# A mixture-of-experts stage on Trainium2: five weight buffers in place of six, and table work moved around the token copies

## What is computed

```
proj = rmsnorm(x) @ w_in
x = x + concat(o_a, o_b, o_c) @ w_out
h = rmsnorm(x)                        # router, then for every expert e:
a = h @ w_e_gate[e]; u = h @ w_e_up[e]
out = out + (silu(a) * u * gate[:, e]) @ w_e_down[e]
return rmsnorm(x + out)
```

## Time and profile before

| | us |
|---|---|
| median of 3 runs | 1177.11 |
| lowest and highest of them | 1172.47, 1177.11 |
| the profiled execution's own time | 1175.49 |
| its span | 1173.7 |

### The profile page before, as it was taken

The page is one execution under the profiler, slowest core; times in us unless marked ns, Lnnn a source line. Parts: engine busy times, 40 slices in busy tenths (PEclk is TensorE's granted clock), DMA queues, the critical chain, the costliest instruction groups (busy, mean ns, idle before and its releaser), DMA issues.

```text
span 1173.7 us, 30645 instructions
## 1 busy us (share of the span) xinstructions
PE 1073.7 (91%) x12370; PEld 912.3 (78%) x12370; DVE 664.3 (57%) x1727; ACT 462.8 (39%) x790; POOL 252.0 (21%) x476
## 2 busy tenths in 40 slices
PE   6999899999999999999999899987989999999980
PEld 5989788778788888888877677777778878888860
DVE  5340445324666666665687533467877755656654
ACT  6321112222455555554587422221334434434333
POOL 1030000000333323321176300001223222323310
PEclk9999899999999999999999999996999999999995
DMA  9020855353656855565332365438899799999927
GB/s 366 20 90 2 292 179 161 108 159 141 160 118 164 205 141 119 127 138 130 105 86 57 120 216 191 135 126 321 285 342 368 229 371 357 356 375 366 366 53 293
DMA packets 77834, 232.92 MB, mean 198 GB/s; under 512 B 23264, under 2 KB 24064, under 8 KB 76544
## 3 DMA queue, kind: packets, MB, share of 16 engines
q1 hardware_dynamic: 70080, 214.18, 55.1%
q0 software_dynamic: 7616, 16.80, 6.3%
HBM read 194.87 MB, written 45.88 MB: 205 GB/s over the span
## 4 chain that ended last, share of the span: by engine, by line
PE 76%; DMA 8%; DVE 6%; issue 4%; ACT 2%; SPq 2%; POOL 1%; POOLq 0%; DVEq 0%; ACTq 0%
PE PS L2382 14%; PE PS L2044 13%; PE PS L2222 9%; PE PS L2306 8%; PE PS L2393 7%; PE PS L2033 6%; PE PS L2200 4%; PE PS L2161 4%; PE PS L2201 3%; DMA wdn<-in_wdn 2%; PE PS L2373 2%; DMA k<-T_d 2%; DMA wst<-in_wt 1%; PE PS L2079 1%; PE PS L2194 1%
## 5 line engine op out<-in xcount | busy, mean ns | idle before, releaser
L2382 PEld LDWEIGHTS PS<-XT,wgu 128*64 128x64 f32 x4352 | 184.9, 139 | 31.0 <-issue 29.1
L1158 ACT ACTIVATE pt<-PS,cst 128x512 f32<-128x512 f32 (+3 forms) x288 | 167.2, 650 | 105.5 <-PE PS L2201 83.3
L2382 PE MATMUL PS<-XT,wgu 128*64 128x96 f32 x4352 | 192.1, 249 | 16.7 <-issue 13.0
L1488 DVE CUSTOM_DVE_ANT_0 junkm<-PS,cst 128x512 f32<-128x512 f32 (+3 forms) x276 | 133.5, 531 | 75.2 <-PE PS L2161 73.0
L2222 PEld LDWEIGHTS PS<-V,pt 128*64 128x64 f32 x3840 | 121.2, 137 | 22.8 <-issue 11.6
L2222 PE MATMUL PS<-V,pt 128*64 128x65 f32 x3840 | 136.8, 225 | 0.7 <-issue 0.7
L2044 PE MATMUL PS<-hTh,wth 128*128 128x512 f32 x256 | 103.0, 402 | 4.8 <-DVE wtl L1335 4.8
L2044 PE MATMUL PS<-hTh,wtl 128*128 128x512 f32 x256 | 100.7, 393 | 0.0
L2044 PE MATMUL PS<-hTl,wth 128*128 128x512 f32 x256 | 100.7, 393 | 0.0
L870 POOL TENSOR_SCALAR_AFFINE_SELECT pt<-pt 128x128 f32<-128x128 f32 x224 | 64.0, 292 | 159.7 <-ACT pt L1158 116.7
L1912 DVE TENSOR_TENSOR wdl<-wdn,wdh 128x1024 fp32r<-128x1024 f32 x64 | 75.5, 1222 | 38.6 <-ACT wdh L999 38.6
(11 more groups left out here) (314 smaller groups left out, 1885.8 us busy)
## 6 DMA issues: line engine op xcount, KB each, us to landing
wgu<-in_wgu SPq DMA_DIRECT2D x32, 2048.0 KB
wdn<-in_wdn SPq DMA_DIRECT2D x32, 1024.0 KB
q<-T_d SPq DMA_DIRECT2D x58, 256.0 KB, 4.3
k<-T_d SPq DMA_DIRECT2D x58, 256.0 KB, 5.5
wst<-in_wt SPq DMA_DIRECT2D x16, 512.0 KB, 6.5
T_d<-thi SPq DMA_DIRECT2D x16, 512.0 KB, 2.7
T_d<-tlo SPq DMA_DIRECT2D x16, 512.0 KB, 3.9
xt<-in_x SPq DMA_DIRECT2D x8, 512.0 KB, 11.3
```

Of the source, the lines that this page charges most:

```text
L1158: ins = nc.scalar.activation(pt[:, (n + 2) % 6, 0:nt * P], PS[:, n % 3, 0:nt * P], ACT.Exp, scale=C("slopes", h, h + 1), bias=C("kb", w, w ...
L1488: V_.tensor_tensor_reduce(out=junk_[:, 0:L], in0=PS[:, bank, 0:L], in1=tab, scale=1.0, scalar=-3e38, op0=ALU.add, op1=ALU.max, accum_out=m ...
L2382: ins = mm(PS[h * HD:(h + 1) * HD, 2 + p, f * CAP:(f + 1) * CAP], wgu[q][:, c, lo:lo + HD], XT[:, p, c, :], start=(c == 0 and f == 0), sto ...
```

## The change

- `RING` goes from 6 to 5: the sixth buffer is gone, `SLOT` is `l % 5` for all loads, and each load from 5 on waits for the down product five loads back. No load waits for `wrow_ov` any more.
- In `m_gate` the copy `m_x(n+1)` stands right behind the clamp, ahead of the wait for the exponential.
- `choose_hosts` stands ahead of `m_x(0)` and not behind it. `count_rest` moves from ahead of tile 0 to behind tile 2. The operation `moved` is taken out of `swap_ids` and stands ahead of tile 0. `swap_ids` and `swap_weights` move one tile ahead. `overflow_places` is cut in two (`tile_steps`, `rank_steps`), and all overflow tables behind it move one tile back, with PE's 16 matmuls two tiles back (behind tile 11).
- On SP the load of 1 MB, not that of 2 MB, stands ahead of the last store of `h2_d`, and the 1 MB of load 3 now waits for the first gather like its 2 MB.

```diff
-RING = 6
+RING = 5
-SLOT = [l % 5 if l < 13 else (5, 3, 4, 0, 1, 2)[(l - 13) % 6] for l in range(NE)]
+SLOT = [l % 5 for l in range(NE)]
...
                 if t + 1 == NT:
                     sp_.wait_ge(g_mm, 2 * NT)
-                    load_up(2, TILE[2]).then_inc(we_in[2], 16)
+                    load_down(2, TILE[2]).then_inc(we_in[2], 16)
                 h2_store(t, p)
 
-            load_down(2, TILE[2]).then_inc(we_in[2], 16)
+            load_up(2, TILE[2]).then_inc(we_in[2], 16)
+            sp_.wait_ge(xg_in[0], 16)
             load_down(3, TILE[3]).then_inc(we_in[3], 16)
-            sp_.wait_ge(xg_in[0], 16)
             load_up(3, TILE[3]).then_inc(we_in[3], 16)
             sp_.wait_ge(h_lg, 8)
             load_expert(TILE[4], 4)
             for l in range(5, NE):
-                if PREV[l] is None:
-                    sp_.wait_ge(dve_did, DV.of("wrow_ov"))
-                else:
-                    sp_.wait_ge(m_dn, DONE[PREV[l]] + 1)
+                sp_.wait_ge(m_dn, DONE[PREV[l]] + 1)
...
                 V_.tensor_scalar(out=ge[:], in0=gate, scalar1=MIN_ARG, scalar2=None, op0=ALU.max).then_inc(m_cl, 1)
-                if n == 0:
-                    m_x(1)
+                if n < NB - 1:
+                    m_x(n + 1)
                 dve.wait_ge(m_e, n + 1)
                 chain(V_.tensor_scalar(out=gd[:], in0=ge[:], scalar1=1.0, scalar2=None, op0=ALU.add))
                 chain(V_.reciprocal(out=gd[:], in_=gd[:]))
-                if 1 <= n < NB - 1:
-                    m_x(n + 1)
...
+            choose_hosts()
             m_x(0)
-            choose_hosts()
             first_weights()
-            count_rest()
+            m_split_lo(0)
+            moved_columns()
             for n in range(NB):
                 m_gate(n)
-                if n == 0:
-                    m_split_lo(0)
                 if n + 1 < NB and LOAD[n + 1] != LOAD[n]:
                     m_split_lo(LOAD[n + 1])
+                if n == 0:
+                    swap_ids()
                 if n == 1:
-                    swap_ids()
+                    swap_weights()
                 if n == 2:
-                    swap_weights()
+                    count_rest()
...
```

More of the change, by code:

```diff
@@ L373, in program @@
         wgu = [at(f"wgu{q}", [P, KC, 2 * DE], f32, o)
-               for q, o in enumerate((ZE + 8 * KB, ZB, ZD, ZD + 24 * KB, ZB + 32 * KB, ZC))]
-        WDN = (dead, ZB + 16 * KB, ZD + 16 * KB, ZD + 40 * KB, ZB + 48 * KB, ZC + 16 * KB)
+               for q, o in enumerate((ZE + 8 * KB, ZB, ZD, ZD + 24 * KB, ZB + 32 * KB))]
+        WDN = (dead, ZB + 16 * KB, ZD + 16 * KB, ZD + 40 * KB, ZB + 48 * KB)
         wdn = [at(f"wdn{q}", [P, 2, D], f32, o) for q, o in enumerate(WDN)]
@@ L562, in program @@
                        "pf0", "f0", "pf1", "f1", "d1", "c1", "c1a", "there", "d2", "c2", "c2b", "place_e", "w_hi", "wrow",
-                       "hosts", "rest", "restv", "vp"]
+                       "moved", "idf", "id_by", "id_at", "idp", "w_by", "w_at", "wrp", "hosts", "rest", "restv", "vp"]
                     + [f"s{k}" for k in (1, 2, 4, 8, 16)]
-                    + ["eb", "idf", "moved", "id_by", "id_at", "idp", "w_by", "w_at", "wrp",
[1 row of a table removed]
[1 row of a table added]
                        "rs", "p1", "p2", "sl", "r", "shf", "shi", "slo",
@@ L1809, in _, with moved_columns @@
             over_e = lambda x: x.unsqueeze(1).unsqueeze(1).broadcast_to([x.shape[0], 4, 6, NE])
+            def moved_columns():
+                tt("moved", moved[0:CAP], late_(con2[0:CAP]).unsqueeze(3).broadcast_to([CAP, 4, 6, NE]),
+                   over_e(fi32[0:CAP]), ALU.is_equal)
             def swap_ids():
                 D_("idf", V_.tensor_copy(out=dv_[0:CAP], in_=ids[0:CAP, 0:NE]))
-                tt("moved", moved[0:CAP], late_(con2[0:CAP]).unsqueeze(3).broadcast_to([CAP, 4, 6, NE]),
-                   over_e(fi32[0:CAP]), ALU.is_equal)
                 tt("id_by", picked[0:CAP], moved[0:CAP], over_e(dv_[0:CAP]), ALU.mult)
@@ L1822, in swap_weights, with tile_steps @@
                 D_("wrp", V_.tensor_copy(out=late_(wrow[0:CAP, 0:NE]), in_=by_group(pf[0:CAP])[:, :, 0:6]))
-            def overflow_places():
-                over_t = lambda x: x.unsqueeze(1).broadcast_to([P, NT, NE])
+            over_t = lambda x: x.unsqueeze(1).broadcast_to([P, NT, NE])
+            def tile_steps():
                 D_("not_h", V_.tensor_scalar(out=not_h, in0=hosts, scalar1=-1.0, scalar2=1.0, op0=ALU.mult, op1=ALU.add))
@@ L1832, in overflow_places, with rank_steps @@
                 D1("z2c", z2, z2, ALU.mult, float(CAP))
+            def rank_steps():
                 D1("ge", rb[:], rank, ALU.is_ge, float(CAP))
@@ L1922, in m_out @@
                                  scalar2=None, op0=ALU.mult).then_inc(m_y1, 1)
+            choose_hosts()
             m_x(0)
-            choose_hosts()
             first_weights()
-            count_rest()
+            m_split_lo(0)
+            moved_columns()
             for n in range(NB):
                 m_gate(n)
-                if n == 0:
-                    m_split_lo(0)
                 if n + 1 < NB and LOAD[n + 1] != LOAD[n]:
                     m_split_lo(LOAD[n + 1])
+                if n == 0:
+                    swap_ids()
                 if n == 1:
-                    swap_ids()
+                    swap_weights()
                 if n == 2:
-                    swap_weights()
+                    count_rest()
                 if n == 3:
-                    overflow_places()
+                    tile_steps()
                 if n == 4:
+                    rank_steps()
+                if n == 5:
                     places()
-                if n == 5:
+                if n == 6:
                     tiles_rows()
-                if n in (6, 7):
-                    tile_columns(n - 6)
-                if n == 8:
+                if n in (7, 8):
+                    tile_columns(n - 7)
+                if n == 9:
                     overflow_rows()
-                if n == 9:
+                if n == 10:
                     overflow_experts()
-                if n == 10:
+                if n == 11:
                     overflow_ids()
```

## The result

The changed kernel takes 1159.17 us (median of 4 runs, 1155.71 to 1161.4), the kernel before 1177.11: a ratio of 0.985, 95% interval 0.982 to 0.9875. The profiled execution of the change took 1155.71 us, the shortest of its four, and its span is 1154.0; the rows of before come from one of 1175.5 with a span of 1173.7.

The account below looks back on a forecast made before the run. PE, busy 91% of the span, was taken as the bound, with 18.7 us of waits as the budget. Terms -5.65 + 0.2 - 2.2 + 2.0 = -5.65 us took 1175.5 to 1169.8 us; range 1165 to 1177.

Parts of the forecast that it names:

- The copy behind the clamp: DVE's copy to `XT`: the five PE waits ahead of up products go, -5.65 us; -2.8 if half stay.
- Table parts: DVE's overflow tables in the expert stage: the moved parts fit between split and clamp and cost nothing.
- Hosts ahead of the first copy: DVE ahead of tile 0: the 20 host operations now precede the first copy, +0.2 us.
- Last store, loads: SP ahead of the first gather: store and gather come sooner, hidden behind the hosts; 0, bounds -0.2 and +0.2 us.
- Five buffers: Weight loads: load 13 issued near 899, DMA hole closes, waits at tiles 13 to 15 go, -2.2 us; PE not starved.
- What comes instead: PE inside an up product near 920 us: full DMA brings back a missing instruction fetch stall, +2.0 us, bounds 0 and 3.7.
- Rival A: PE near 920 us: no new fetch stall, 1167.8 us, or 1166.2 without the clock's fall near 1092; chance 0.20.
- B: PE's up products: fetch stalls eat the gain, with fewer pauses to catch up; sum -0.65, 1174.8 us; chance 0.15.
- C: Copy to `XT`: still late, DVE or ACT keeps half of the five waits, 1172.6 us; chance 0.13.
- D: Late tiles' weight loads: five buffers starve PE, 1176 us at 11.25 us a load, 1185.5 at 11.6; chance 0.10.

Follow-up runs that it names:

- a3_old_sp: The changed kernel with the old order of loads on SP: 1159.18 us, ratio 0.985 to the kernel before.
- e2_ring5: The kernel before with only five buffers and no wait of load 13 for the overflow tables: 1171.81 us, ratio 0.997.
- a2: The changed kernel with six buffers and the wait of load 13 for the overflow tables: 1168.87 us, ratio 0.994 to the kernel before.
- e6: The kernel before with the early copy, five buffers and the new order on SP, tables as they were: 1157.09 us, ratio 0.984.

## Why the prediction was wrong, and where it held

**"The copy behind the clamp" held.** All five waits went (5.95 us by intervals, 5.65 by rows), the copy ends 0.8 us behind the clamp's start where 1.05 was worked out, and no table part made it late.

**"Table parts" and "Hosts ahead of the first copy" held in the sum.** The clamp of tile 1 came at 822.16 behind `swap_ids`, and nothing on PE waited for it. From the last projection to the first up product it takes 23.15 us, not 22.97: the +0.2 that was forecast.

**"Last store, loads" held**, as a term of 0: a3_old_sp. That it is worth 3 us without the hosts was implied by "hidden behind the hosts" but not priced.

**"Five buffers" held in direction and place.** Load 13 was issued at 896.70 ("near 899"), the hole is gone, and PE is not starved: SP waits 130.6 us between 860 and 1100 for buffers, while the DMA stays full. The sum took -2.2 and the stage shows -1.65, since one new weight wait of 0.7 appeared at tile 22. Its real weight was not seen: with the tables one tile later, six buffers would have cost 9.7 us.

**"What comes instead" is the step that failed.** It took +2.0 us: the border waits stay as they are, and full DMA engines near 920 add one. The runs put -7.4 for the waits and -1.7 for the lower clock behind the 2.03 one in its place, -9.1 in all. The 11.1 us between +2.0 and -9.1 are nearly the whole gap between -5.85 and -17.55. The last up product came at 1109.4, not near 1122.8. The wait at 920 does come when the buffers alone are changed (2.57 us in e2_ring5). The flaw lay in taking the border waits as a property of the DMA's load alone. They hang as much on how early a fetch starts, and this on when the sequencer is let go. The prediction did not look at that, though it stands in the source view of PE's semaphore wait. Moving the copy changed exactly that by 1.67 us. In the kernel before, the next q8 packet started 3.5 us behind a border (median of 38) and 6 us or more behind eleven of them; in the change 2.8 us, and 6 or more behind two.

The Trainium skill, Runtime: NRT & Kernel Launch, section Instruction fetch mechanics, says that fetches run ahead and stay hidden. Rival A used it: no new wait near 920. There it was right, for the change as a whole. As a rule it does not hold in any of these runs: the border waits sum to between 2.2 and 13.1 us a run, with PE otherwise ready.

**The rivals.** B (borders eat the gain) looked at the right item and had its sign wrong: PE's pauses ahead of up products were not what let fetches catch up. Where they went, the border waits shrank. C and D did not happen: no wait of more than 0.7 us on `XT`, one of 0.7 us on `wdn`. No rival had the existing border waits go, although the sum of rows made them the largest item of the budget, 9.4 of 18.7 us. An item of that size that one part of the change might touch deserved a bound below zero; the prediction bounded only the new wait, and only from 0 up.

**What stays open.** That the sequencer asks for a block sooner when it is let go sooner is a reading of when the packets start; the request itself is in no view. Why some borders wait and others don't was found in part: in the kernel before, the groups of waits begin at borders that fall in the transposes (851.4, 961.1, 1017.9 and 1074.8 us), and the next packet starts 6.3 to 9.6 us behind each of these. Why such a packet is later, and why the waits of tiles 22 and 23 stay in the early-copy kernels (in a2 and e6 only that of 23), was not found. Nor is each size safe to a us: every border sum here comes from one execution.

## What to carry to other kernels

And price a change as a whole: the parts here sum to 6 us of gain one by one and give 18 together, mostly because five buffers and the late tables meet in one wait of SP.

## What the runs showed of the hardware that had not been expected

- Waits at borders of 256 instructions: up to 2.57 us each with the DMA engines full, 11.05 us over 33 tiles in the kernel before, 3.65 in the change. They end 1.2 to 1.6 us behind the landing of the 16 KB packet.
- Scatters are close to their pace in the change. POOL waits 165.1 us for the scatter before (27 times, 806 to 1120 us) where it waited 57.9 us (16 times, the same window), and no wait of PE in the stage names the scatters.
- A wait of this kind can cost twice: behind the 2.57 us of e2_ring5 the granted clock was at its lower level (0.51 is 1.2 GHz, 1.00 is 2.4), after the engine had stood for that time. The 2.04 us wait of the change at 1020.8 had no such effect: the 38 matmuls behind it took 1.81 us. In a3_old_sp a wait of 1.82 us, over at 1013.1, had it: the clock was at its lower level (0.50) from 1014.8 for 3.4 us. So the length of the wait alone does not tell. The windows of e2_ring5 (the third column from the end is the clock):

```profile
921.00:922.00 1.00, 1.00 (x18) 1.00 (x16) 0.00 (x0) 0.00 (x0) 0.00 (x0) 0.51 0.99 283
...
925.00:926.00 1.00, 1.00 (x6) 0.72 (x5) 1.00 (x1) 0.44 (x1) 0.30 (x1) 1.00 1.02 406
```
